# Attention scores of 64- and 32-row heads as three fp32r products on the heads' own array rows, two heads side by side

## The reference, cut to what matters

```python
s_w = jnp.einsum('bcqgrd,bckgd->bcgrqk', qb, kb).astype(f32) * scale      # NSA window; the selected branch alike
s_w = jnp.where(mask_w[None, :, None, None], s_w, NEG)
p_w = jax.nn.softmax(s_w, axis=-1).astype(vb.dtype)
...
sc = jnp.einsum('bhcqd,bhckd->bhcqk', qi, k).astype(jnp.float32) * scale  # differential, DIFF_DIM = 32
sc = jnp.where(k_pos <= q_pos, sc, NEG_INF)
p = jax.nn.softmax(sc, axis=-1)
a = p[:, :, 0] - lam * p[:, :, 1]
```

## Time and profile before

| | |
|---|---|
| runs | 2212.74, 2214.19, 2214.22 us; median 2214.19 us |
| the profiled execution | 2214.59 us, of which the profile's span is 2212.8 us |
| PE, DVE, ACT, POOL busy | 98%, 68%, 43%, 54% of the span |
| granted TensorE clock | 0.995 of full speed over the span |
| NSA scores on PE (line 1560, kT_n) | 128 records, from 210 to 299 us |
| scores of the later layers | 320 records, from 1034 us and up to 1784 us |

### The profile page before, as it was taken

The page is one execution under the profiler, slowest core; times in us unless marked ns, Lnnn a source line. Parts: engine busy times, 40 slices in busy tenths (PEclk is TensorE's granted clock), DMA queues, the critical chain, the costliest instruction groups (busy, mean ns, idle before and its releaser), DMA issues.

```text
span 2212.8 us, 33023 instructions
## 1 busy us (share of the span) xinstructions
PE 2160.8 (98%) x12331; PEld 1840.0 (83%) x12331; DVE 1500.5 (68%) x2224; ACT 944.2 (43%) x1882; POOL 1189.3 (54%) x582
## 2 busy tenths in 40 slices
PE   6999999999999999999999999999999999999997
PEld 4788888877899988887887898888897887888885
DVE  6834877554666692897646776677896728777676
ACT  3254663011556610644743555412555725455311
POOL 4747403776477677745016644577653037444673
PEclk9999999999999999999999999999999999999999
DMA  8422102422133333232002222322221012222221
GB/s 318 156 73 86 62 30 88 181 94 96 58 115 115 109 142 135 77 115 77 1 4 92 96 91 100 115 95 84 107 93 61 1 39 86 92 90 115 95 95 57
DMA packets 32776, 206.78 MB, mean 93 GB/s; under 512 B 4080, under 2 KB 4336, under 8 KB 11632
## 3 DMA queue, kind: packets, MB, share of 16 engines
q1 hardware_dynamic: 32192, 200.27, 24.9%
q10 hardware_dynamic: 432, 4.46, 0.5%
HBM read 202.61 MB, written 2.10 MB: 93 GB/s over the span
## 4 chain that ended last, share of the span: by engine, by line
PE 87%; DVE 8%; DMA 1%; DVEq 1%; issue 1%; ACT 1%; POOL 1%; POOLq 0%; SPq 0%; ACTq 0%
PE PS L1118 18%; PE PS L1120 18%; PE PS L1119 18%; PE PS L1560 5%; PE PS L1572 5%; PE PS L1375 3%; PE PS L1373 3%; PE PS L1374 3%; PE PS L1586 3%; PE PS L1449 2%; PE PS L1451 2%; PE PS L1450 2%; DMA raw<-slabs_dram 1%; DVE PS L3374 1%; PE PS L1132 1%
## 5 line engine op out<-in xcount | busy, mean ns | idle before, releaser
L665 POOL TENSOR_TENSOR w_hi<-raw,zero_c 128x512 fp32r<-128x512 f32 (+1 forms) x135 | 279.5, 2088 | 546.2 <-PE PS L1120 544.8
L669 POOL TENSOR_TENSOR w_lo<-raw,w_hi 128x512 fp32r<-128x512 f32 (+1 forms) x135 | 367.4, 2740 | 5.8
L1118 PE MATMUL PS<-b_hi,w_hi 128*128 128x512 f32 x528 | 209.8, 397 | 1.0 <-POOL w_lo L888 1.0
L1119 PE MATMUL PS<-b_lo,w_hi 128*128 128x512 f32 x528 | 209.3, 396 | 0.0
L1120 PE MATMUL PS<-b_hi,w_lo 128*128 128x512 f32 x528 | 209.3, 396 | 0.0
L3288 DVE TENSOR_TENSOR b_lo<-a_all,b_hi 128x512 fp32r<-128x512 f32 x44 | 162.5, 3732 | 49.4 <-ACT b_hi L2446 49.4
L1118 PE MATMUL PS<-f_hi,w_hi 128*128 128x512 f32 x448 | 177.6, 397 | 0.7 <-DVE f_lo L2590 0.7
L1120 PE MATMUL PS<-f_hi,w_lo 128*128 128x512 f32 x448 | 177.6, 396 | 0.0
L1119 PE MATMUL PS<-f_lo,w_hi 128*128 128x512 f32 x448 | 177.6, 396 | 0.0
L688 POOL TENSOR_TENSOR w_lo<-raw,w_hi 128x512 fp32r<-128x512 f32 x48 | 71.0, 1479 | 93.6 <-ACT w_hi L2438 93.6
L1118 PEld LDWEIGHTS PS<-b_hi,w_hi 128*128 128x128 f32 x528 | 99.5, 188 | 25.6 <-POOL w_lo L888 1.2
(11 more groups left out here) (570 smaller groups left out, 6822.3 us busy)
## 6 DMA issues: line engine op xcount, KB each, us to landing
raw<-slabs_dram SPq DMA_DIRECT2D x161, 1024.0 KB, 4.8
aux<-ada_dram SPq DMA_DIRECT2D x18, 512.0 KB, 5.0
ada_first<-ada_dram SPq DMA_DIRECT2D x11, 512.0 KB, 13.9
cmpw<-cmpw_dram ACTq DMA_DIRECT2D x2, 2048.0 KB, 11.7
ada_late<-ada_dram SPq DMA_DIRECT2D x8, 512.0 KB, 3.3
ada_last<-ada_dram SPq DMA_DIRECT2D x8, 512.0 KB, 5.8
xT<-xT_dram SPq DMA_DIRECT2D x1, 2048.0 KB, 9.2
out_dram<-t SPq DMA_DIRECT2D x4, 512.0 KB, 2.7
```

Of the source, the lines that this page charges most:

```text
L665: high = nc.gpsimd.tensor_tensor(w_hi[:, slot, c], raw[:, slot, c], zero[:, 0:c.stop - c.start], ALU.add)
L669: low = nc.gpsimd.tensor_tensor(w_lo[:, slot, c], raw[:, slot, c], w_hi[:, slot, c].bitcast(f32), ALU.subtract)
L1118: nc.tensor.matmul(out, a_hi_, b_hi_, start=start, stop=False)
L1119: nc.tensor.matmul(out, a_hi_, b_lo_, start=False, stop=False)
```

## The change

Queries and keys of the 64- and 32-row heads are split in fp32r parts when they leave PSUM (ACT writes the high part, then DVE the low part, for every item; the masks are gone). A score tile is three fp32r matmuls on the head's own rows of the array (64, or 32 for a differential map): high by high, high by low, low by high. One of nb = 1 is made 256 columns wide. The NSA jobs are reordered so that the two groups' heads follow each other, and their tiles, like those of two dilated heads or of the two maps of a differential head, are issued together: the first product of one, the first of the other, and so on, in the first one's step. The waits of both tiles come ahead of the six matmuls. Plain heads keep one tile at a time (in the order 1, 0, 3, 2), with three matmuls. Two mated heads share an output bank and are finished together after the second one's last values product. MLA heads are unchanged. Some tiles move in SBUF, and the high part of O2 lies in two places.

```diff
@@ class Plan
-                    group = [m + 1, m] if m + 1 < len(jobs) and is_pair(jobs[m + 1]) else [m]
+                    woven = m + 1 < len(jobs) and is_pair(jobs[m + 1])
+                    group = [m + 1, m] if woven else [m, m + 1] if jobs[m]["mate"] else [m]
+                    for i, g in enumerate(group):
+                        if jobs[m]["mate"]:
+                            self.home[g] = (6 + mates % O_BANKS, TT * HD * i)
...
+                        self.finishes[g] = () if jobs[g]["mate"] else (g - 1, g) if jobs[m]["mate"] else (g,)
...
+                        if jobs[m]["mate"] or woven:
+                            self.together[at0] = (at0, at0 + 1)
@@ job tables
+            for b in (1, 2):
+                for g in range(GROUPS):
...
+                    nsa_jobs.append(job(((qT_split[:, 2 * r, :], qT_split[:, 2 * r + 1, :]),),
+                                        (kT_hi[:, b - 1, :], kT_lo[b - 1][:]), v,
...
+                                        rows=(slice(64 * g, 64 * g + 64),), mate=g == 0))
...
-        def apart(n, src, slots, masks):
-
-            parts = [(slots[i], masks[:, i:i + 1]) for i in range(masks.shape[1])]
-            return (src, P, parts, []) if n % 2 == 0 else (src, P, [], parts)
+        def split_turn(src, homes, scale):
+
+            hi, lo = homes
+            return (src, P, [(hi, scale)], [(lo, hi, scale)])
@@ PE, attend
-                        if step >= s_banks:
-                            pe.wait_ge(scores_masked, g0 + step - s_banks + 1)
-                        nc.tensor.matmul(PS[:, step % s_banks, 0:128 * nb], query_tile(jobs[m]["q"][c], j),
+                    for i in plan.together.get(step, ()):
...
+                        if i >= s_banks:
+                            pe.wait_ge(scores_masked, g0 + i - s_banks + 1)
...
+                    elif step in plan.together:
+                        for part, (of_q, of_k) in enumerate(((0, 0), (0, 1), (1, 0))):
+                            for i in plan.together[step]:
+                                m, c, j, _ = plan.scores[i]
+                                lo, nb = key_range(jobs[m], j)
+                                rows_, wide = jobs[m]["rows"][c], max(2, nb)
+                                last = nc.tensor.matmul(PS[:, i % s_banks, 0:128 * wide],
+                                                        key_tiles(jobs[m]["q"][c][of_q], rows_, j, 1),
+                                                        key_tiles(jobs[m]["k"][of_k], rows_, lo, wide),
+                                                        start=part == 0, stop=part == 2)
+                                if part == 2:
+                                    last.then_inc(scores_ready, 1)
@@ DVE, attend
                         if v in plan.last:
-                            m = plan.values[v][0]
                             dve.wait_ge(pv_done, v0 + v + 1)
-                            finish(jobs[m], m, plan.sums[m][0] % 8)
+                            for m in plan.finishes[plan.values[v][0]]:
+                                finish(jobs[m], m, plan.sums[m][0] % 8, plan.home[m])
@@ DVE, take_turned (two_taken alike)
+                dve.wait_ge(nsa_act, NSA_HIGH[n])
+                hi, lo, scale = nsa_split(n)
+                V.scalar_tensor_tensor(out=lo, in0=PS[:, bank, :], scalar=scale, in1=hi.bitcast(f32), op0=ALU.mult,
+                                       op1=ALU.subtract).then_inc(nsa_dve, 1)
```

More of the change, by code:

```diff
@@ L1003, in key_range, with job @@
             return lo, j - lo + 1
[L1005 to L1006 removed]
+        def job(q, k, v, out, strip=None, window=False, coef=None, mode="set", turned_by=None, vector=True, rows=None,
+                mate=False):
+            return dict(rows=rows, mate=mate, vector=vector, q=q if isinstance(q, tuple) else (q,), k=k, v=v, out=out, strip=strip, window=window, coef=coef, mode=mode, turned_by=turned_by)
         def sigm(h, b):
@@ L1041, in build @@
-            two_jobs.append(job((diff_q[2 * h], diff_q[2 * h + 1]), T2b[:, 2 + h // 2, :],
+            other = h + 1 - 2 * (h % 2)
+            two_jobs.append(job((plain_q[other // 2],), plain_k[other // 2],
+                                lambda kb, h=other: z2[:, 2, kb, 256 + 64 * h:320 + 64 * h],
+                                O2[:, :, 512 + 64 * other:576 + 64 * other], causal, vector=False,
+                                rows=(half_rows(other),)))
+            two_jobs.append(job((diff_q[h // 2], diff_q[h // 2]), diff_k[h // 2],
@@ L1549, in attend @@
                 for step in range(plan.steps):
-                    if step < n:
+                    for i in plan.together.get(step, ()):
+                        m = plan.scores[i][0]
+                        if banks_ready:
+                            banks_ready(i)
+                        if jobs[m]["turned_by"] and i % TT == 0:
+                            pe.wait_ge(mla_act, jobs[m]["turned_by"])
+                            pe.wait_ge(mla_dve, jobs[m]["turned_by"])
+                        if i >= s_banks:
+                            pe.wait_ge(scores_masked, g0 + i - s_banks + 1)
@@ L1551, in attend @@
+                    if step in plan.together and jobs[plan.scores[step][0]]["rows"] is None:
                         m, c, j, _ = plan.scores[step]
                         lo, nb = key_range(jobs[m], j)
-                        if banks_ready:
-                            banks_ready(step)
-                        if jobs[m]["turned_by"] and step % TT == 0:
-                            pe.wait_ge(mla_act, jobs[m]["turned_by"])
-                            pe.wait_ge(mla_dve, jobs[m]["turned_by"])
@@ L1568, in attend @@
                         pe.wait_ge(*copies[v])
-                        if v in plan.first and m >= O_BANKS:
-                            pe.wait_ge(out_used, m0 + m - O_BANKS + 1)
+                        if v in plan.first and plan.prior[m]:
+                            pe.wait_ge(out_used, m0 + plan.prior[m])
+                        bank, col0 = plan.home[m]
                         for b in range(nb):
-                            last = nc.tensor.matmul(PS[:, 6 + m % O_BANKS, 64 * j:64 * j + 64],
+                            last = nc.tensor.matmul(PS[:, bank, col0 + 64 * j:col0 + 64 * j + 64],
                                                     turned_slot(ring, v, 512)[:, 128 * b:128 * b + 128],
@@ L2172, in _, with nsa_high @@
                 latent_squares(0, z[:, 2, tt, :], tt)
-            for n in (0, 2):
+            def nsa_high(n, bank):
                 act.wait_ge(nsa_turned, n + 1)
-                for dst, scale in nsa_parts(n):
-                    A(dst, PS[:, n, :], ACT.Copy, scale=scale).then_inc(nsa_act, 1)
+                hi, _, scale = nsa_split(n)
+                A(hi, PS[:, bank, :], ACT.Copy, scale=scale).then_inc(nsa_act, 1)
+            for n in range(REP):
+                nsa_high(n, n)
+                if n % 2 == 0:
+                    A(qT_u[:, n, :], PS[:, n, :], ACT.Copy, scale=-HD ** -0.5).then_inc(nsa_act, 1)
             act.wait_ge(ck_turned, 1)
             A(c_kkT[:], PS[:, 0, 0:N_PAIR], ACT.Copy).then_inc(ckk_ready, 1)
+            nsa_high(REP, 1)
             act.wait_ge(c_shifted, 1)
@@ L2239, in _ @@
             q_squares(1)
-            for tt in (1, 2, 3):
+            take_kv(1)
+            nsa_high(REP + 1, 3)
+            for tt in (2, 3):
                 take_kv(tt)
```

152 lines of the change are left out of this document (84 added, 68 removed).

## The result

The change takes 2323.69 us (median of four runs, 2322.44 to 2328.91) against 2214.2 for the kernel before in the same job: a ratio of 1.050, interval 1.048 to 1.052. It is 110 us slower, where 2193.5 was forecast and the range ended at 2232. The profiled execution took 2328.91 us, 114 of span more than before.

A forecast was written before the change was run, and what follows sets the result against it. PE was taken to bound the kernel, busy 98% of the span. Its gain of 26.6 us, less 4 and 2 given back, is 20.6: from 2214.6 to 2194, as median 2193.5 us; range 2170 to 2232.

The forecast's parts named there:

- wrong altogether: Closing condition: granted clock under 1.00 in the three stages, or new copies delaying step 0; no size given.
- Two heads share the array: Score groups: two heads' products run together, a pair at one tile's price, 0.70, 0.52, 0.35, 0.35 us.
- Rival C: Groups of six: the two heads' products run one after the other; 2235 us, chance 0.25.
- rival B: Score groups: weight loads of both heads come one after the other; 2217 us, harsher form about 2230; chance 0.15.
- Change of rows 0.25 us: Each score group: going from 128 rows to fewer and back costs 0.25 us, ends 0.05 and 0.35; 128 groups.
- rival A: Score groups: changes of rows nearly free, 0.05 us a group; 2172 us, chance 0.20.
- Plain heads alone cost more than before: Later layers' single plain heads: 2.92 us on PE against 2.16 before, a loss of 0.76 each.
- Given back in the NSA stage, 4 us, up to 12: NSA stage: PE waits for masks behind double finishes on DVE, up to 1.5 us a pair; 4 us taken.
- 1 us in each: Each later layer: 1 us given back for ACT's and DVE's two extra operand copies; double finish short.
- Copies at the turns cost nothing: Query and key copies at the turns: as many as before on the whole, nothing charged.
- each low part now follows a high part: Copies at the turns: new order of the split parts; window keys take about 1.3 us, missed 3.4 us later.
- The gain of 26.6 us on TensorE: Score products at full clock: 10.2 us in the NSA stage, 8.2 in each of two later layers.

The follow-up runs named there:

- on all rows: The change with each score product on all 128 rows instead of the head's own 64 or 32; 2260.99 us.
- the run with own rows alone: The kernel before with its fp32 score products on the head's own 64 or 32 rows, nothing else changed; 2410 to 2538 us.
- one tile on all rows: The change with woven jobs as before, each tile of a pair in its own step, three products on all 128 rows; 2237.6 us.
- the woven stage as before: The change in the NSA and dilated stages only, woven jobs with their masked fp32 operands as in the kernel before; 2253.83 us.
- the run with one tile on its own rows: The change with woven jobs as before, each tile of a pair in its own step, three products on the head's own 64 rows; 2393.33 us.

## Why the prediction was wrong

**The step that failed** is in its first paragraph: "The granted clock is 1.00 in all, so the array runs at the 2.4 GHz level and nothing is to be had there." Nothing was to be had, but much was to be lost, and every price of the sum was taken at 1.00. The clock was named only at the end, as what would make the forecast "wrong altogether", with no rival, no chance and no price. It fell to 0.50, and the woven stage took 92.9 us where 51 to 52 were forecast; the same products on all rows kept 1.00 and took 61.2. The price was in reach of the rows: at half the clock TensorE's 51.8 us of the woven stage become up to twice that, 104 us more for two layers. What the trace of before could not show is that few rows bring it about. The Trainium skill, page TensorE: Matmul & The Clock Gate, section What's actually happening, has the clock follow how busy TensorE has been lately. By that rule it would have stayed up in the run with own rows alone, where TensorE was busy 20.00 of 20.00 us at 0.50; the measurement decides.

The account of the 110 us, by medians: 70 for the change in the woven stages (2323.7 - 2253.8); 20 for pairing (2237.6 - 2217.2); 3 for split copies and products (2217.2 - 2214.2); 16 for the step from one tile on all rows to two on their own (2253.8 - 2237.6), where a gain was forecast. They are steps from one kernel to the next, so that they add up says nothing for their names. Of the woven stages' part, few rows are the most, net of what side by side saves: 31.7 us in the first layer's stage (92.9 - 61.2) and 30.3 in the second's (91.6 - 61.3), while 7.7 and 7.8 stay on all rows. The 16 hold the gain of TensorE, new waits for two masks at once and short falls of the clock, and are not separated further; the two profiled executions are only 5 us apart (2244.97 and 2239.88).

Point by point:
- *Two heads share the array:* right. At the full clock a group of two blocks takes 0.55 us (forecast 0.60), of three 0.72 (0.77), of four 0.89 (0.95); the two heads' first products start less than 0.01 us apart. On all rows the same groups take 0.79, 1.13 and 1.47. Rival C did not come true, and rival B's 0.97 neither.
- *Change of rows 0.25 us:* right within 0.06; rival A's 0.05 would have given 0.57 for three blocks.
- *Plain heads alone cost more than before:* right in sign, and far worse than 0.76 us a head: 1.58, 1.26, 0.94 and 0.94 us a tile at half the clock, 4.7 in place of 2.16. The differential groups, 32 rows beside 32, use as few rows, and no run tells the two apart.
- *Given back in the NSA stage, 4 us, up to 12:* mis-sized. The mechanism was right (the double finish, the wait for the tile two before), but it reaches TensorE by ScalarE too, and standing still brought falls of the clock, which no term has. On all rows the groups wait 59.7 us for masks in the three kinds of stage together.
- *"1 us in each" later layer:* wrong. At a nearly full clock the pairs in the later layers lost, too: of the 30 us of span that the profiled execution with the woven stage as before lost, the NSA stage had 9 (98.3 against 89.1 us from first to last score) and the rest was in the layers.
- *Copies at the turns cost nothing:* right on balance, together with the products of the NSA and dilated stages at most 5 us (1.0003 to 1.0023). The woven stages' 3.7 us each are not nothing; "each low part now follows a high part" was seen for step 0 and for the window keys, and stands in the trace within the woven stage.
- *The gain of 26.6 us on TensorE:* right for a group at the full clock, where two full maps take 0.89 + 0.72 + 0.55 + 0.55 = 2.7 us (forecast 2.92, before 4.32), and lost at half of it, where they take 4.7. No whole stage shows it. With the woven stage as before the NSA windows have TensorE busy 87.17 of 99.00 us, where it was 87.30 of 89.50 before:

```profile
210.00:309.00 99.00, 87.17 (x659) 70.33 (x657) 67.66 (x239) 58.56 (x179) 32.22 (x27) 0.93 0.17 59
```

```profile
210.00:299.50 89.50, 87.30 (x602) 72.74 (x601) 70.85 (x248) 59.05 (x183) 32.21 (x27) 1.00 0.18 64
```

What side by side saves was spent at a clock of 0.93, and TensorE stands still for 12 us where it was 2. The Trainium skill, page TensorEngine Tiling (Array Packing), section PSUM Bottleneck, warns that the engines that empty PSUM may become the limit once TensorE is faster. The trace agrees in part: score products wait 23.1 us for VectorE's masks in the change and 1.0 before, but 59.7 on all rows, where no head shares the array with another, so the pairing brings such waits even without the packing.

## What to carry to other kernels

Before products are moved onto part of the array's rows, price the stage at half the clock and give that case a chance: it costs up to the stage's TensorE time again, more than any product saved here. Where TensorE is busy without a gap while PEclk reads 5, look at the rows in use before the number of products: here 192 useless ones on all rows took 43 us off. Read the clock by windows, too; the row of 40 slices hid falls to 0.84. Pairing two streams on one engine also pairs the work that others do for them: count the bursts on VectorE, and follow them through ScalarE.

## What the hardware showed that was not expected

- The granted clock sat at 0.50 with TensorE busy without a gap, for as long as scores used 32 to 64 rows (93 us in the woven stage, 100 in the run with one tile on its own rows), although every values product and transpose between them used 128. On all rows the woven stage held 1.00 with TensorE idle for 9 of 61 us.
- Short falls came on all 128 rows as well, where pairs made TensorE stand still (0.94 in most of the NSA stage, 0.91 in the dilated one), about as deep as with pairs on their own rows (0.93 and 0.90).
- It came back as the share of products on all rows rose: not with one more a group, fully with three.
- Six products of two heads took 0.72 us whether they were written by turns or one head after the other (0.17 us a product of 384 columns: three in the time of six). The Trainium skill, page TensorE: Matmul & The Clock Gate, section The mechanism (of packing small matmuls), has matmuls start strictly in program order; then the second head should have begun after the first head's third product had started, 0.34 us later. The trace disagrees: it has the second head's first product 0.01 us behind the first head's. It doesn't tell where the order was changed.
- With own rows, the same program took from 2410 to 2538 us; of all others the slowest was within 1% of the fastest.
